# Adaptive modulation in four groups, a third level buffer, and a reordered entry into the up-projection

## The reference

```
sh1, sc1, gt1, sh2, sc2, gt2 = (silu(cond) @ w_ada + b_ada) split in 6       # per condition: latent and context
h  = rmsnorm(x, g_mix) * (1 + sc1) + sh1
gq, gk, gv, gr, zf, zb, nq, nk, nv, m_gla, m_na = split(h @ w_in)
la_f, la_b = log_sigmoid(zf @ w_af + b_af) / 16, log_sigmoid(zb @ w_ab + b_ab) / 16
b_gla = (rmsnorm(gla_bidir(gq, gk, gv, la_f, la_b)) * silu(gr)) @ w_gla_o     # chunked linear attention, 2 directions
b_na  = neighbourhood_attention(norm(nq), norm(nk), nv, cached k, cached v, rpb) @ w_na_o
x  = x + gt1 * ((sigmoid(m_gla) * b_gla + sigmoid(m_na) * b_na) @ w_out)
h2 = rmsnorm(x, g_ffn) * (1 + sc2) + sh2
a, g = split(conv3(h2 @ w_up) + b_conv)                                       # depthwise over tokens, D_FF = 2816
x  = x + gt2 * ((a * silu(g)) @ w_down)
```

## Time and profile before

| | |
|---|---|
| median of 3 runs | 1088.03 us (1086.72 to 1089.21) |
| the profiled execution | 1087.97 us, its span 1086.2 us |
| PE, busy | 1028.5 us, 95% |
| DVE / ACT / POOL, busy | 588.3 / 434.6 / 483.4 us |
| granted TensorE clock, mean over the span | 0.984 |

### The profile page before, as it was taken

One profiled execution on the slowest core, in us unless ns is written; L12 is line 12 of the kernel. 1 busy time (PEld: TensorE's weight loads), 2 busy tenths in 40 slices (PEclk: granted clock), 3 DMA queues, 4 the chain that ended last, 5 costly groups with the idle time before them and its releaser, 6 DMA issues.

```text
span 1086.2 us, 19005 instructions
## 1 busy us (share of the span) xinstructions
PE 1028.5 (95%) x7419; PEld 944.7 (87%) x7419; DVE 588.3 (54%) x1059; ACT 434.6 (40%) x675; POOL 483.4 (45%) x296
## 2 busy tenths in 40 slices
PE   4899999899899999999999978999999999999998
PEld 4789999898698888999988878999999999688886
DVE  5524039994566563233253797777777777731102
ACT  3242252332656664222231454555545555521110
POOL 2164631351522131232244146788887876333331
PEclk9889999999999999999999988999999999999999
DMA  9766222112100112746634112222233321222231
GB/s 353 242 78 98 72 64 59 40 40 59 49 19 23 40 40 79 245 153 210 207 129 166 39 40 79 78 79 78 79 87 98 88 79 40 78 78 75 72 115 68
DMA packets 126603, 103.64 MB, mean 95 GB/s; under 512 B 5790, under 2 KB 102851, under 8 KB 126531
## 3 DMA queue, kind: packets, MB, share of 16 engines
q1 hardware_dynamic: 121568, 95.11, 28.6%
q0 software_dynamic: 1504, 3.15, 2.1%
q10 hardware_dynamic: 3459, 4.40, 1.2%
HBM read 98.18 MB, written 3.41 MB: 94 GB/s over the span
## 4 chain that ended last, share of the span: by engine, by line
PE 59%; POOL 18%; DVE 12%; issue 3%; ACT 3%; DVEq 0%; POOLq 0%; ACTq 0%
PE PJ L588 9%; POOL behind L550 8%; PE PJ L589 8%; PE PJ L593 8%; POOL ahead L550 5%; PE PA L956 3%; PE PA L958 3%; PE PA L957 3%; PE PJ L956 3%; PE PJ L958 3%; PE PJ L957 3%; POOL behind_val L558 2%; POOL ahead_val L558 2%; PE PA L894 2%; DVE A L1771 2%
## 5 line engine op out<-in xcount | busy, mean ns | idle before, releaser
L453 POOL TENSOR_TENSOR wlo<-wraw,whi 128x1024 fp32r<-128x1024 f32 x73 | 192.8, 2643 | 362.4 <-ACT whi L1132 266.2
L588 PE MATMUL PJ<-h_hi,whi 128*128 128x320 f32 x640 | 199.1, 319 | 5.8 <-DVE h_lo L1647 5.0
L589 PE MATMUL PJ<-h_lo,whi 128*128 128x320 f32 x640 | 195.7, 314 | 0.0
L593 PE MATMUL PJ<-h_hi,wlo 128*128 128x320 f32 x640 | 148.1, 313 | 0.0
L588 PEld LDWEIGHTS PJ<-h_hi,whi 128*128 128x128 f32 x640 | 122.9, 192 | 8.7 <-issue 6.7
L1132 ACT ACTIVATE whi<-wraw 128x1024 fp32r<-128x1024 f32 x52 | 54.8, 1055 | 174.5 <-PE PJ L593 92.1
L589 PEld LDWEIGHTS PJ<-h_lo,whi 128*128 128x128 f32 x640 | 122.9, 192 | 0.0
L593 PEld LDWEIGHTS PJ<-h_hi,wlo 128*128 128x128 f32 x640 | 109.4, 192 | 0.0
L1490 ACT ACTIVATE whi<-wraw 128x1024 fp32r<-128x1024 f32 x21 | 22.2, 1059 | 110.0 <-PE PJ L958 56.6
L2052 DVE SCALAR_TENSOR_TENSOR PJ<-u_all,vec,PJ 128x641 f32<-128x641 f32 x44 | 39.2, 890 | 48.7 <-ACT PJ L1448 48.7
L1076 PE MATMUL PA<-h_hi,behind 128*128 128x320 f32 x192 | 59.3, 309 | 0.0
(11 more groups left out here) (425 smaller groups left out, 2858.7 us busy)
## 6 DMA issues: line engine op xcount, KB each, us to landing
wraw<-in_w_in_dram SPq DMA_DIRECT2D x82, 256.0 KB, 3.1
ada_rest<-in_w_ada_dram SPq DMA_DIRECT2D x32, 512.0 KB, 5.6
wraw<-in_w_up_dram SPq DMA_DIRECT2D x48, 256.0 KB, 3.3
wraw<-in_w_down_dram SPq DMA_DIRECT2D x44, 256.0 KB, 2.8
raw_even<-in_w_up_dram SPq DMA_DIRECT2D x40, 256.0 KB, 3.7
ada_lo_half<-in_w_ada_dram SPq DMA_DIRECT2D x4, 1024.0 KB, 9.6
ada_hi_half<-in_w_ada_dram SPq DMA_DIRECT2D x4, 1024.0 KB, 15.5
wraw<-in_w_out_dram SPq DMA_DIRECT2D x16, 256.0 KB, 3.2
```

Source lines behind the costliest of these rows:

```text
L453: pool.tensor_tensor(wlo[:, slot, 0:k, :], wraw[:, slot, 0:k, :], whi[:, slot, 0:k, :].bitcast(F32), ALU.subtract).then_inc(lo_done, 1)
L588: pe.matmul(out, whi[:, slot, w0 + k, :], hi(k)[:, tok], start=start and k == k0, stop=False)
L589: pe.matmul(out, whi[:, slot, w0 + k, :], lo(k)[:, tok], start=False, stop=False)
L593: mm = pe.matmul(out, wlo[:, slot, w0 + k, :], hi(k)[:, tok], start=False, stop=stop and k == k1 - 1)
```

## The change

Four parts, independent of each other in the code.

1. **Start and gates.** The modulation comes in four groups of two channel blocks, scale and shift together, each from its own buffer. The transposes have a third bank pair (PA). The first tile's 32 gate columns are written four times over, so that z fills 64 rows. The first three tiles are computed block by block side by side, the third into PA. The weights of the third tile are split at the start. The tiles that follow change their places with the gates: the next tile, the transposes of the cached keys, one more tile, the first pair of gates, a tile, the second pair. The gate matmuls of a pair stand in different groups of 32 rows.
2. **Levels.** A third buffer `lvl2`; the arguments and exponentials of levels 1 and 2 stand ahead of the copies of `v_tok`; each of a level's six pieces has a bank of its own, PA's four and one pair of PJ. So attention tiles 2 to 9 all use the other pair of PJ, each only after the tile before it has been copied out, and ACT copies before it makes the next `whi`.
3. **Transition.** POOL's `first_tokens` waits for the last normalization of DVE and is split in four pieces; `pair_lo` is made one step sooner; two waits of PE are gone; the order of DVE and ACT changes.
4. **End of the up-projection.** The first three `act_low_part` move behind the sums of the last cycle but one, `act_low_part(3)` and `conv(21, 1)` change places with what stood about them, ACT makes parts 3 and 4 sooner, and the first down-projection tile takes the token tiles in the order 4, 0, 1, 2, 3.

```diff
+        def level_of(n):
+
+            return (lvl[:, 0], lvl[:, 1], lvl2[:, :, :])[(n + 1) % 3]
+
+        def level_bank(j):
+
+            return PA[:, j * BANK:(j + 1) * BANK] if j < 4 else PJ[:, (j - 2) * BANK:(j - 1) * BANK]
...
+            def ada_group(g):
+
+                for part in range(2):
+                    at_ = part * D + g * 256
+                    sp.dma_start(ada[g][:, :, part * 256:part * 256 + 256], w_ada_v[:, :, at_:at_ + 256]).then_inc(ada_in[g], 16)
+
+            chunk(0, 0, w_in_v, IN_Z, None)
+            ada_group(0)
+            chunk(1, 0, w_in_v, 0, None)
+            ada_group(1)
+            chunk(0, 0, w_in_v, P, 1)
+            ada_group(2)
+            ada_group(3)
...
-            lo(0, 1)
+            pool.wait_ge(xn_set, NT)
+            pool.wait_ge(hi_done, 1)
+            pool.tensor_tensor(fourfold(wlo), first_rows(wraw), fourfold(whi).bitcast(F32), ALU.subtract).then_inc(lo_done, 1)
             lo(1, 2)
-            pool.wait_ge(xn_set, NT)
-            pool.dma_start(kc_tok[:, :, :], cache_k[0, 0].rearrange("(b p) h d -> p b (h d)", p=P)).then_inc(past_in, 16)
-            pool.dma_start(vc[:, :, :], cache_v[0, 0].rearrange("(b p) h d -> p b (h d)", p=P)).then_inc(past_in, 16)
-            pool.wait_ge(const_set, 4)
-            pool.dma_start(w_alpha[0:16, 0:256], w_af[0]).then_inc(past_in, 16)
-            pool.dma_start(w_alpha[16:32, 256:512], w_ab[0]).then_inc(past_in, 16)
-            pool.wait_ge(hlo_set, 4)
             pool.wait_ge(hi_done, 3)
             pool.tensor_tensor(third_lo[:, :, :], wraw[:, 0, :, :], third_hi[:, :, :].bitcast(F32), ALU.subtract).then_inc(lo_done, 1)
+            pool.wait_ge(hlo_set, 4)
...
+                for k in range(k0, k0 + 4):
+                    ins = pool.tensor_tensor(h2f[:, k, span], h_hi[:, k, span].bitcast(F32), h_lo[:, k, span].bitcast(F32), ALU.add)
+                ins.then_inc(pooled_set, 1)
 
             def pair1_low(slot):
 
@@ -535,10 +573,11 @@
 
             pool.wait_ge(x2_set, 2 * NT)
             pool.wait_ge(h2lo_set, NK)
+            pool.wait_ge(x2n_set, NT)
             first_tokens(0)
             pair1_low(1)
+            pair1_low(0)
             first_tokens(4)
-            pair1_low(0)
...
+            for k in range(NK):
                 for n in range(2):
-                    first_tiles(n, (k,))
-
-            pe.wait_ge(tile_freed, 1)
-            project(0, 3, hh, hl, PJ, 0, done=tile_ready, whi=third_hi[:, :, :].unsqueeze(1), wlo=third_lo[:, :, :].unsqueeze(1))
-            pe.wait_ge(past_in, 64)
-            pe.wait_ge(mod_set, 4)
+                    first_tile(n, k)
+                if k % 2 == 0 and k < 6:
+                    rows_to_columns(k // 2 + 1)
+                if k in (1, 3):
+                    for past in (k - 1, k):
+                        first_tile(2, past)
+                    modulation_rows(k // 2 + 2)
+            for k in range(4, NK):
+                first_tile(2, k)
+
+            pe.wait_ge(tile_freed, 2)
+            project(1, 4, hh, hl, PJ, 1, done=tile_ready)
...
+            gate_pair(0)
+            pe.wait_ge(tile_freed, 4)
+            project(1, 6, hh, hl, PJ, 1, done=tile_ready)
+            gate_pair(1)
...
+                pe.wait_ge(tile_freed, n - 1 if a < 2 else n)
+                if a == 10:
+                    pe.wait_ge(lv_cp, NT + 6 * N_LEVEL)
+                project(n % 2, n + 1, hh, hl, PJ, attention_pair(a), done=tile_ready)
...
-            pe.wait_ge(ev_set, 1)
             project(1, C_UP + 3, hh, hl, PA, 0, done=up_ps, whi=pair1_hi, wlo=pair1_lo)
-            pe.wait_ge(ev_set, 2)
             project(0, C_UP + 4, hh, hl, PA, 1, done=up_ps, whi=pair1_hi, wlo=pair1_lo)
...
+            act.wait_ge(raw_in[0], 64)
+            act.activation(third_hi[:, :, :], wraw[:, 0, :, :], ACT.Copy).then_inc(hi_done, 1)
...
+                hi(n % 2, (n + 2) // 2 + 1)
+                if 2 <= a < 9:
+                    level_exp(a + 1)
...
-                    product_done("P5", m)
-                    wide_in(0)
                     product_done("P7", m)
                     act_high_part(3)
+                    act_high_part(4)
+                    wide_in(0)
...
+            args(1)
+            args(2)
             for t in range(NT):
                 dve.wait_ge(vt_ps, t + 1)
-                copied(dve.tensor_copy(v_tok[:, t, :], PA[:, bank():bank() + BANK]))
+                dve.tensor_copy(v_tok[:, t, :], level_bank(t % 4)).then_inc(lv_cp, 1)
+            decayed(1)
+            decayed(2)
             dve.wait_ge(mask_in, 32)
-            for n in range(1, N_LEVEL + 2):
-                args(n)
-                if n <= N_LEVEL:
-                    score_copy(n - 1)
-                decayed(n)
+            for n in range(N_LEVEL):
+                score_copy(n)
+                if n:
+                    decayed(n + 2)
+                if n + 3 < N_LEVEL + 2:
+                    args(n + 3)
...
+            second_sum(2)
             conv(0, 1)
             dve.wait_ge(h2t_set, 2 * NK + 4)
             t_low(1)
+            second_low(2)
             conv(0, 0)
             gate_product(0)
-            second_sum(2)
+            fourth_sum(2)
             t_low(2)
-            second_low(2)
-            fourth_sum(2)
...
+                if c == NF:
+                    act_low_part(3)
+                    conv(c - 1, 1)
...
+                if c == NF - 1:
+                    for k in range(3):
+                        act_low_part(k)
+                elif c < NF:
                     conv(c, 1)
```

More of the change, by code:

```diff
@@ L1095, in _ @@
                 w_hi, w_lo = (wide(w) for w in ((whi[:, slot, :, :], wlo[:, slot, :, :]) if n else (first_hi, first_lo)))
-                for t in range(NT):
+                for t in range(NT) if n else (4, 0, 1, 2, 3):
                     if n == 0:
-                        pe.wait_ge(add_set, ADDED[("U2", "U3", "C21", "C12", "C11")[t], NF - 1])
+                        pe.wait_ge(add_set, ADDED[("U3", "C21", "C12", "C11", "U2")[t], NF - 1])
                     if n == 11 and t == 0:
@@ L1202, in _ @@
[L1202 to L1208 removed]
+                if n >= 4:
+                    log_gates(n - 4)
+            with act.Fori(0, 3) as i:
                 for b in range(2):
[L1210 to L1212 removed]
+                    act.wait_ge(tile_ready, i * 2 + (b + 7))
+                    hi(b, i + 5)
+                    act.activation(by_half(U[:, bass.ds(i * 2 + (b + 5), 1), :].rearrange("p a n -> p (a n)")), halves(PJ, b), ACT.Copy)\
@@ L1538, in _ @@
                 else:
-                    for k in range(4, 6):
-                        act_high_part(k)
+                    act_high_part(5)
                 unit_high(m + 1, "S4", "P3")
@@ L2171, in _ @@
                     near_sum("U2", c, "P6", ua[:, c % 2, near], tmp[:, :])
-                if c == NF - 1:
-                    for k in range(3):
-                        act_low_part(k)
                 second_sum(c + 1)
```

337 lines of the change are left out of this document (159 added, 178 removed).

## The result

The changed kernel takes 1077.51 us in the median of five runs (1076.60 to 1080.84), the kernel before 1087.91 us beside it: a ratio of 0.9909, with a 95% interval from 0.9892 to 0.9927. The forecast was 1078.0. The profiled execution took 1077.69 us.

The account below looks back on a forecast made before the run. PE, busy 95% of 1086.2 us, was taken to bound the kernel, so gains come only from its waits and half clock. Start -2.0, levels -7.0, transition -3.5 and end +2.5 sum to -10.0: 1078.0 us, range 1070.5 to 1084.

Parts of the forecast that it names:

- The levels: Attention levels: with six separate banks the eight waits of PE go, -7.0 us, ends -5.0 and -7.5.
- The start: First tiles and gates: earlier first product and cheaper gates, less a new wait for low weights, -2.0 us, ends +1 and -5.
- the stall: Near 66 us PE waits about 7.3 us for POOL's low weights, which stand behind the bias DMAs.
- R3: Rival, start: POOL's bias DMAs do not stop it, start term -6 or -8, about 1073 us, chance 0.12.
- R5: Rival, slower: POOL's low weights behind stretched DMA issue make the start's tiles wait, 1089 to 1092 us, chance 0.06.
- R4: Rival, small gain: DVE paces the levels (-3), start 0, transition -2, 1085 or 1083 us, chance 0.17.
- The transition: Into the up-projection: 3.0 us from the normalization and 0.5 from the order of sums, -3.5 us, ends -2 and -9.
- the ring: Up-projection: DVE, ACT and POOL set the pace, 12.69 us a cycle; only what brings them forward counts.
- R2: Rival: the up-projection follows PE (-9) and the end costs nothing, 1070 us, chance 0.20.
- The end: Start of the down-projection: `act_low_part` meets POOL's `first_lo` and delays the tiles, +2.5 us, ends +4 and -1.5.
- allowance of 0.3 for half clock: Start of the down-projection: one chance in five of another 1.65 us at half clock, counted as 0.3.
- B: The term for the attention levels: the eight waits for banks go, -7.0 us.

Follow-up runs that it names:

- start_third_later: The changed kernel, but ACT makes the third tile's high weights behind the high parts of blocks 0 and 1, not ahead of them: 1073.27 us, ratio 0.9874.
- end_wide_early: The changed kernel with the three `act_low_part` moved back and ACT making the second down-projection tile's high weights ahead of the last silu: 1074.88 us, ratio 0.9874.
- best_two: The changed kernel with `third_hi` later, POOL's low weights ahead of bias waits at two places, `act_low_part` back, second down-projection tile's high weights early: 1062.64 us, ratio 0.9758.

## Why the prediction was right

**The levels** are the safe term: -7.37 against -7.0. They were counted from waits that stood in the trace, with one releaser, and the new waits were looked for on the queues behind them. In all ten profiled executions with six banks and three buffers the stretch is 89.34 or 89.35 us.

**The start** was 1.8 us too good (-0.18, not -2.0), and the step that failed is the first product: forecast 29.0, measured 31.0. The landing of the third chunk was nearly right (26.2 forecast, 26.61). Missed was what it releases: `third_lo` on POOL started 0.6 us ahead of DVE's `h_lo` and held it for 1.6 us. Both stood in queues that were read, but only the queues were, not who runs beside whom. The late product went through to level 0 because the landing of the bias rows, which the forecast held fixed, moved with it, as `start_third_later` confirms: the low weights behind them were forecast for 73.3, and PE has them at 74.9. The size of the stall came near what was reckoned (7.3 forecast, 6.56 measured), as did the gates (1.3, 1.35). That stall rules out R3, a stall no longer than forecast R5, and the -7.37 of the levels R4.

**The transition** was mis-sized the other way: -5.98, not -3.5. The mechanism is the one forecast (the ring starts sooner, its period stays, PE's earlier product is worth nothing: 16.6 us there, 12.4 at the ring), and R2 with it is out. The terms were 3.0 for POOL's wait and 0.5 for the order. By the runs the wait alone gives 1.5, the order 1.4, and 2.2 come from what was counted at nothing: the same edit cuts POOL's long instruction in four, and that shortens DVE's `h_lo` behind it. I had named the pieces only as a risk. The last 0.8 stay open.

**The end** costs 0.91, not 2.5. The collision is there (3.70 us for three pieces), and the first tile waits for it: in every profiled execution with this order it starts 0.1 us behind the second piece. Yet counted from `conv(1, 0)` the first tile comes 0.24 us later than before, not 1.2, because `first_lo`, beside which the pieces wait, itself ran 0.85 us sooner (ACT's `first_hi` waited 0.65 us for its weights, not 2.83). From the first tile to the second it is 9.36 us; 8.69 were measured before and 9.7 forecast. That forecast laid the chain through DVE's last convolutions to the second tile's low parts. But the second tile takes parts 2 and 3, and the change itself had put part 3 ahead of the convolutions; it waits 0.67 us for its low weights, whose high weights come late on ACT, and `end_wide_early` removes that wait. The allowance of 0.3 for half clock was for nothing, though the half clock came: `wlo` is what the second tile waits for at either clock. (One slip in the working: with 3022 ns for the first piece the three end near 924.6, not 924.2; the first tile needs two, so its 924.0 is hardly touched.)

**Not forecast at all** is the stretch to the fourth normalization, +1.10, of which about 1.0 is the half clock at 286 us; the change does not touch this code. The errors are +1.8 and +1.1 on one side, -2.5, -1.6 and -0.4 on the other, and another +1.0 lies around the span; so the errors cancelled, and that only 0.5 us lie between 1078.0 and 1077.51 is luck. Of the four terms only B was right in size.

## What to carry to other kernels

Waits of one engine for one releaser can be added up, and in the levels their removal paid in full, because the queues of the engines that take over had been followed. An instruction that is made early costs nothing only if no operand of it is late: `third_hi`, early in ACT's queue for a tile that came last, held the first tile, and cost 5 us. A `wlo` that PE needs soon belongs ahead of the DMAs that wait, not behind them (6.0 us), and before a second buffer is added it is worth asking whether the wait is for the buffer or for the bank.

## What the runs showed of the hardware

**Half clock does not follow from the wait alone.** Three waits of PE that are equal within 0.02 us in all thirteen profiled executions were followed by it in some: 2.0 us ahead of line 901 (853 before) in 8 of 13, 2.54 us for `rin_wide` in 9, 1.92 us for `row_diag` in 7. The stretch from the keys to the fourth normalization, which holds all three and is the same code in every kernel, took from 368.3 to 372.9 us (in the longest, `best_two`, the half clock behind the first of the three lasts 6.8 us; in the others that drew it there, 3.4). So a gain under some 2 us has to be read from stretches of the trace, not from single times.

**DVE beside POOL.** The wait of a DVE instruction goes by how much of POOL's instruction is left: `h_lo` of 128x256 takes 0.42 us alone, 0.6 to 0.9 beside pieces of 128x384, 2.0 beside a `pair_lo` of 128x1024, up to 3.10 beside one of 128x1536 (at 638.94 us in the kernel before). The pieces cost POOL itself 9.0 us in place of 7.1, which here nobody waits for. The Trainium skill ("SBUF — State Buffer", "Who interferes with whom") has an exclusive lock of the pair of ports that DVE shares with GpSimd, held for a whole instruction. The trace agrees: at 28.32 us `h_lo` took 2.45 us, the 1.77 that were left of POOL's instruction and 0.7 more; and cutting POOL's instruction shortened the wait.

**Gates in two row groups.** Eight matmuls of 32 rows by 320 columns took 1.35 us in pairs on different groups, 2.42 in one: 1.8 times as fast.
